# Attention's turn by row halves with values in pairs, and feed-forward's hidden block split ahead

## The reference

```
h = rmsnorm(x); z = h @ w_in          # q, k, v, forget of group A; q, k, v of group B
s = einsum(q, k) * SCALE + bias       # A: causal, bias C[t] - C[s], C = cumsum(log sigmoid(f))
p = softmax(s)                        # B: own chunk of 64 and 8 chunks before, bias by distance
o = einsum(p, v)                      # 8 heads of 64 in each group
x = x + rmsnorm(concat(rmsnorm(oa), rmsnorm(ob)) @ w_out)
hf = rmsnorm(x)
x = x + rmsnorm((silu(hf @ w_gate) * (hf @ w_up)) @ w_down)    # 1024 -> 2816 -> 1024
```

## Time and profile before

| | us |
|---|---|
| median of 3 runs | 3740.98 (3739.13 to 3746.12) |
| profiled execution | 3741.29 |
| its span | 3739.6 |
| PE busy | 3186.6 (85%) |
| weight loads busy (beside PE) | 2799.0 (75%) |
| DVE busy | 1498.0 (40%) |
| ACT busy | 1228.9 (33%) |
| POOL busy | 188.6 (5%) |

### The profile page before, as it was taken

One profiled execution on the slowest core, in us unless ns is written; L12 is line 12 of the kernel. 1 busy time (PEld: TensorE's weight loads), 2 busy tenths in 40 slices (PEclk: granted clock), 3 DMA queues, 4 the chain that ended last, 5 costly groups with the idle time before them and its releaser, 6 DMA issues. The chain is left out here.

```text
span 3739.6 us, 55132 instructions
## 1 busy us (share of the span) xinstructions
PE 3186.6 (85%) x21766; PEld 2799.0 (75%) x21766; DVE 1498.0 (40%) x2841; ACT 1228.9 (33%) x1920; POOL 188.6 (5%) x167
## 2 busy tenths in 40 slices
PE   0599999907999999745796999899899899899898
PEld 0499999806777767523585899799799799799797
DVE  4300000046656677512443443443443434434454
ACT  3111111105666667411443322222222222222333
POOL 4100000000000000000010000100100100100100
PEclk9999999958999999868898999999899999999999
DMA  2111111123211122297454334234333433433454
GB/s 96 65 71 68 70 69 46 37 36 121 67 57 31 33 76 61 68 313 277 142 162 156 131 128 158 101 125 174 105 121 137 146 118 134 146 123 129 152 185 146
DMA packets 176471, 428.39 MB, mean 115 GB/s; under 512 B 14952, under 2 KB 100512, under 8 KB 155808
## 3 DMA queue, kind: packets, MB, share of 16 engines
q1 hardware_dynamic: 154920, 399.40, 31.8%
q10 hardware_dynamic: 21392, 26.82, 2.0%
HBM read 361.45 MB, written 64.71 MB: 114 GB/s over the span
## 5 line engine op out<-in xcount | busy, mean ns | idle before, releaser
L172 PE MATMUL ffn_pg<-ffn_hh,ffn_wgh 128*128 128x384 f32 (+1 forms) x1056 | 350.7, 332 | 119.3 <-DVE ffn_hl L1662 119.3
L1590 ACT ACTIVATE ffn_wdh<-ffn_wdr 128x1024 fp32r<-128x1024 f32 x132 | 140.0, 1060 | 930.2 <-PE ffn_py L1551 930.2
L1652 DVE TENSOR_TENSOR ffn_wgl<-ffn_wgr,ffn_wgh 128x2048 fp32r<-128x2048 f32 x132 | 313.3, 2374 | 90.9 <-ACT ffn_wgh L1584 90.9
L174 PE MATMUL ffn_pg<-ffn_hh,ffn_wgl 128*128 128x384 f32 (+1 forms) x1056 | 349.6, 331 | 0.0
L173 PE MATMUL ffn_pg<-ffn_hl,ffn_wgh 128*128 128x384 f32 (+1 forms) x1056 | 349.1, 331 | 0.0
L172 PE MATMUL ffn_pu<-ffn_hh,ffn_wgh 128*128 128x384 f32 (+1 forms) x1056 | 343.7, 326 | 0.0
L173 PE MATMUL ffn_pu<-ffn_hl,ffn_wgh 128*128 128x384 f32 (+1 forms) x1056 | 343.7, 326 | 0.0
L174 PE MATMUL ffn_pu<-ffn_hh,ffn_wgl 128*128 128x384 f32 (+1 forms) x1056 | 343.7, 326 | 0.0
L1657 DVE TENSOR_TENSOR ffn_wdl<-ffn_wdr,ffn_wdh 128x1024 fp32r<-128x1024 f32 x132 | 161.8, 1226 | 435.4 <-ACT ffn_wdh L1590 435.4
L172 PEld LDWEIGHTS ffn_pg<-ffn_hh,ffn_wgh 128*128 128x128 f32 x1056 | 203.2, 192 | 126.3 <-issue 74.1
L1550 PE MATMUL ffn_py<-ffn_wdl,ffn_ah 128*128 128x512 f32 x748 | 293.1, 392 | 0.0
(11 more groups left out here) (203 smaller groups left out, 5858.7 us busy)
## 6 DMA issues: line engine op xcount, KB each, us to landing
ffn_wgr<-in_w_gu SPq DMA_DIRECT2D x132, 1024.0 KB, 4.8
ffn_wdr<-in_w_dn SPq DMA_DIRECT2D x132, 512.0 KB, 3.5
att_raw<-out_zT SPq DMA_DIRECT2D x64, 256.0 KB, 2.9
str_kr<-in_cache_ak SPq DMA_DIRECT2D x8, 2048.0 KB, 16.8
str_vr<-in_cache_av SPq DMA_DIRECT2D x8, 2048.0 KB, 15.9
out_zT<-prj_zo ACTq DMA_DIRECT2D x64, 224.0 KB
prj_raw<-in_w_slab SPq DMA_DIRECT2D x12, 1024.0 KB, 5.1
out_v<-prj_vo ACTq DMA_DIRECT2D x68, 128.0 KB, 1.8
```

Of the source, the lines that this page charges most:

```text
L172: nc.tensor.matmul(out, a_hi(k), b_hi(k), start=(k == 0), stop=False)
L174: last = nc.tensor.matmul(out, a_lo(k), b_hi(k), start=False, stop=(k == kk - 1))
L1652: nc.vector.tensor_tensor(wgl[u][:], wgr[u][:], f32(wgh[u][:]), ALU.subtract).then_inc(s_gl, 1)
```

## The change

In attention:
- `attend_order` puts the turn ahead of the scores in each step.
- `turn` takes each 128×128 block in two halves of 64 query rows, x = 0 and 1: each is a transpose with 64×128 weights and 64 moving columns, on rows 64x to 64x+64, into bank pt[x]. Both heads of a half lie in one bank, and the counter s_tr goes up once for a group and no longer once for each head.
- `copy` takes pt[x], both heads at once, into the columns 64x to 64x+64 of each tile in the new pts (3 buffers of 4 KB). DVE takes half 1 of the groups with even G, ACT all others.
- `values` and `turn_out` run only ahead of a turn with even G: the values of two groups one after the other, one and two groups further back than before.
- `turn_out` is two plain fp32 matmuls on column halves.
- On ACT the exponential of the next job's head 1 stands behind both copies of the group with g = 1 (or of the only group). `sums` has 6 buffers.

DVE's order in attention follows PE's in the same way (evict, outward, copy).

In the feed-forward block: hh and hl have two buffers. `walk` is unrolled over the blocks. The high and low halves of block b+1 are made ahead of the last step of block b, its load is issued after the second step of block b, ACT's sums of squares of block b come after the first step of block b+1, and DVE's scaling after its second step. PE waits for the low half in step 0 of a block.

```diff
         done = 0
         for x in range(parts):
             upto = -(-len(scored) * (x + 1) // parts)
+            out += turned[x:x + 1]
             out += scored[done:upto]
             done = upto
-            out += turned[x:x + 1]
     return out
 
 
...
-
-    def by_dve(e, g):
-        return e == 1 and g == 0
-
-    def copies(n, e, g, dve):
-
-        own = sum(by_dve(y, x) == dve for x in range(g + 1) for y in range(2) if (x, y) <= (g, e))
-        return (n if dve else 2 * A0[n] - n) + own
+    NPT, NSX, NSM, NOS, NRAW = 3, 3, 6, 4, 4
+
+    def by_dve(G, x):
+        return x == 1 and G % 2 == 0
+
+    def copies(G, dve):
+
+        return (G // 2 + 1) if dve else 2 * (G + 1) - (G // 2 + 1)
...
-        pts = [[m.sb(f"pts{e}{u}", [P, 512]) for u in range(NPT)] for e in range(2)]
+        pts = [m.sb(f"pts{u}", [P, 2, 4, P]) for u in range(NPT)]
-        sums = [m.sb(f"sums{u}", [P, 2]) for u in range(NSX)]
+        sums = [m.sb(f"sums{u}", [P, 2]) for u in range(NSM)]
...
-                def copied(n, e, g):
-                    if by_dve(e, g):
-                        pe.wait_ge(s_cd, copies(n, e, g, True))
-                    else:
-                        pe.wait_ge(s_ca, copies(n, e, g, False))
-
-                def turn(n, g, before):
+                def copied(G):
+                    pe.wait_ge(s_ca, copies(G, False))
+                    pe.wait_ge(s_cd, copies(G, True))
+
+                def turn(n, g):
+                    G = A0[n] + g
                     tiles = job_groups(n)[g]
                     t0 = job_tiles(n)[0]
+                    if G >= 1:
+                        copied(G - 1)
                     for e in range(2):
                         if g == 0:
                             pe.wait_ge(s_ex, 2 * n + e + 1)
-                        if before:
-                            copied(before[0], e, before[1])
                         for j, kt in enumerate(tiles):
                             c = (kt - t0) * P
-                            last = nc.tensor.transpose(pt[e][:, j * P:(j + 1) * P], sx[n % NSX][:, e, c:c + P], eye[:])
-                        last.then_inc(s_tr, 1)
+                            for x in range(2):
+                                r = slice(64 * x, 64 * x + 64)
+                                to = (4 * e + j) * 64
+                                last = nc.tensor.transpose(pt[x][:, to:to + 64], sx[n % NSX][r, e, c:c + P], eye[r, r])
+                    last.then_inc(s_tr, 1)
...
-                    nc.tensor.transpose(po[n % 2][:, P:2 * P], ot[n % 2][:], eye[:]).then_inc(s_to, 1)
+                    for x in range(2):
+                        r = slice(64 * x, 64 * x + 64)
+                        last = nc.tensor.matmul(po[n % 2][r, P:2 * P], ot[n % 2][:, r], eye[:], start=True, stop=True,
+                                                skip_group_check=True)
+                    last.then_inc(s_to, 1)
...
-                held, ended = None, None
+                held, ended = [], []
                 for what, n, g in ORDER:
                     if what == "score":
                         score(n, g)
                     else:
-                        turn(n, g, held)
-                        if ended is not None:
-                            turn_out(ended)
-                            ended = None
-                        if held:
-                            values(*held)
-                            if last_of(*held):
-                                ended = held[0]
-                        held = (n, g)
-                if ended is not None:
-                    turn_out(ended)
-                values(*held)
-                turn_out(held[0])
+                        if (A0[n] + g) % 2 == 0:
+                            for x in ended:
+                                turn_out(x)
+                            ended = []
+                            for x in held[:-1]:
+                                values(*x)
+                                if last_of(*x):
+                                    ended.append(x[0])
+                            held = held[-1:]
+                        turn(n, g)
+                        held.append((n, g))
+                for x in ended:
+                    turn_out(x)
+                ended = []
+                for x in held:
+                    values(*x)
+                    if last_of(*x):
+                        ended.append(x[0])
+                for x in ended:
+                    turn_out(x)
...
-                    if n >= NSX:
-                        act.wait_ge(s_ev, n - NSX + 1)
+                    if n >= NSM:
+                        act.wait_ge(s_ev, n - NSM + 1)
                     nc.scalar.activation(sx[n % NSX][:, e, :w], sx[n % NSX][:, e, :w], ACT.Exp, bias=nm[n % NSX][:, e:e + 1],
-                                         scale=-1.0, accum_out=sums[n % NSX][:, e:e + 1]).then_inc(s_ex, 1)
...
...
                 for what, n, g in ORDER:
                     if what == "turn":
                         more = n + 1 < NJOB
-                        copy(n, 0, g)
+                        copy(n, g, 0)
                         if more and g == 0:
                             exps(n + 1, 0)
-                        if more and g == 1:
-                            exps(n + 1, 1)
-                        copy(n, 1, g)
-                        if more and g == 0 and last_of(n, g):
+                        copy(n, g, 1)
+                        if more and g == (0 if last_of(n, 0) else 1):
                             exps(n + 1, 1)
                         if last_of(n, g):
...
-        hh = m.sb("hh", [P, KD, TM], F32R)
-        hl = m.sb("hl", [P, KD, TM], F32R)
+        hh = [m.sb(f"hh{u}", [P, KD, TM], F32R) for u in range(2)]
+        hl = [m.sb(f"hl{u}", [P, KD, TM], F32R) for u in range(2)]
...
+        def tiles_of(b):
+            return 3 if b < NBL - 1 else 2
+
+        def walk(eng, step, after_first, after_second, before_last, finish):
+
+            for b in range(NBL):
+                nt = tiles_of(b)
                 step(b, nt, 0, 0)
-                with eng.Fori(0, NJ // 2 - 1) as i:
-                    for u in (1, 0):
-                        step(b, nt, 2 * i + 2 - u, u)
+                after_first(b)
+                step(b, nt, 1, 1)
+                after_second(b)
+                with eng.Fori(1, NJ // 2 - 1) as i:
+                    for u in range(2):
+                        step(b, nt, 2 * i + u, u)
+                step(b, nt, NJ - 2, 0)
+                before_last(b)
                 step(b, nt, NJ - 1, 1)
-                last(b, nt)
-            blk(0, 3)
-            with eng.Fori(1, NBL - 1) as b:
-                blk(b, 3)
-            blk(NBL - 1, 2)
+                finish(b)
+
+        def nothing(b):
+            return None
...
+                def hidden(b):
+                    if b < NBL:
+                        after(sp, s_hl, b)
+                        sp.dma_start(hr[:, :, :tiles_of(b) * P], t["hT"][:, :, b * TM:b * TM + tiles_of(b) * P]).then_inc(s_h, 16)
...
-                walk(sp, first, step, lambda b, nt: None)
+                hidden(0)
+                walk(sp, step, nothing, lambda b: hidden(b + 1), nothing, nothing)
...
+                    if isinstance(j, int) and j == 0:
+                        pe.wait_ge(s_hl, b + 1)
...
+                def hidden(b):
+                    if b < NBL:
+                        w = tiles_of(b) * P
+                        act.wait_ge(s_h, 16 * b + 16)
+                        if b >= 2:
+                            act.wait_ge(s_pu, NJ * (b - 1))
+                        nc.scalar.activation(hh[b % 2][:, :, :w], hr[:, :, :w], ACT.Copy).then_inc(s_hh, 1)
...
+                def sums(b):
+                    if b < 0:
+                        return
...
+                hidden(0)
                 split_gate(0, 0, 0)
                 split_down(0, 0, 0)
-                walk(act, first, step, last)
+                walk(act, step, lambda b: sums(b - 1), nothing, lambda b: hidden(b + 1), evict)
+                sums(NBL - 1)
...
+                def scaled(b):
+                    if b < 0:
+                        return
...
+                hidden(0)
                 split_gate(0, 0, 0)
                 split_down(0, 0, 0)
-                walk(dve, first, step, last)
+                walk(dve, step, nothing, lambda b: scaled(b - 1), lambda b: hidden(b + 1), evict)
+                scaled(NBL - 1)
```

134 lines of the change are left out of this document (60 added, 74 removed).

## The result

| | before | after |
|---|---|---|
| median, us | 3743.14 (4 runs) | 3633.86 (4 runs, 3631.93 to 3640.15) |
| ratio, 95% interval | | 0.9712 [0.9695, 0.9728] |
| profiled execution, its span | 3741.29, 3739.6 | 3640.15, 3638.4 |
| attention of the new stream, first to last matmul | 703.9 | 683.8 |
| from there to the first matmul of the feed-forward | 496.6 | 502.2 |

What follows compares the result with a forecast made beforehand. PE was taken to set the end in both attention and feed-forward. From 3741.3 us, 98 off in the feed-forward and 108 in attention (145 of PE's work less 37 of waits) gave 3535, range 3490 to 3605.

Steps and rivals of the forecast that it cites:

- PE's work: Attention: PE's work falls 145 us: turn −84, switches −47, first loads −28, turn-out +14.
- The price of a half-turn pair: Attention: two half-height transposes cost 0.058 us in place of 0.109, 84 us off over 1648 transposes.
- Rival 1: Attention: two half-height loads go one after another, a pair costs 0.110, turning gains nothing; 3600 us, chance 0.17.
- The strided copies: Attention: strided reads and 256 B pieces cost copies nothing, at most 0.1 us each, 41 us of ACT.
- rival 4: Attention: PE's waits drop the granted clock to 0.50, the stage takes some 950 us, the kernel 3890; chance 0.03.
- What then is late: Attention: of PE's 145 us, 37 come back as waits around copies and exponentials, leaving −108.
- Rival 2: Attention: ACT's chain of copies and exponentials swallows the gain, leaving 30 to 54 us; 3600 us, chance 0.09.
- The six buffers of sums: Attention, jobs of one group: ACT's waits on the output buffer's eviction go, 2.4 us a head pair.
- Boundaries: Feed-forward: PE's waits for the low half go at 5 block boundaries, 89.4 us, plus 0.8 of matmul tail.
- The clock's 7.5 us: Feed-forward: the half-speed clock after each of 5 boundary gaps goes if PE does not stop, 1.5 us each.
- The scaling in step 2: Feed-forward: DVE's moved scaling can make a step late by 0.3 us, 2 in all; left at 0.
- Rival 3: Attention: nothing waits, PE's 145 us come in full and 2 to 10 us of old waits go; 3490 us, chance 0.05.

Runs made afterwards that it cites:

- `full_turn`: The whole change, but with the old 128×128 transposes over the whole array, a head in a bank; 0.9924 of before, 3718 us.
- `evict_between`: The whole change, but DVE evicts an ended job between the two bias passes of the last scores ahead of an even turn; 0.9594 of before.
- `values_apart`: On `between_spread`, one group's values stand ahead of the even turn and the other's behind it; 0.9505 of before, 3560.0 us.
- `half_copy`: On `between_spread`, the second head's half of every copy left out, a timing kernel only; 0.949 of before, 3552 us.
- `exp_behind`: On `evict_between`, both of ACT's copies put ahead of the exponential that stood between them; 0.9599 of before.
- `half_turn`: The kernel before with only the turn by row halves, its order, pairing, sums and feed-forward kept; 0.9965 of before, 3732 us.
- `between_spread`: On `evict_between`, DVE's feed-forward scaling spread over three steps, one row block each, in place of one step; 0.9564 of before.

## Why the prediction was wrong

Two terms of attention failed: PE's work, mis-sized, and above all the waits that it would turn into, one of which was not in the sum.

**PE's work: −145 was too much, about −100 is what the rows show.** Its busy time in the stage fell by 102 us (675.4 to 573.1), and its idle time rose by 81 (25 to 106); their difference is the 21 us that the window lost. The price of a half-turn pair, 0.058 us, is near: in the timeline above four pairs take 0.27 us, 0.11 for the first and 0.06 for each behind it. But the first pair of every group costs that 0.11, so the mean is 0.066 (2983 intervals of 0.033 us within groups, the 33 with a stop in them left out), and the turns gave some 70 us by this estimate, not 84. The change between whole array and row halves is 0.093 as said: a whole transpose is followed by values or scores after 0.202 us (before, `full_turn`) and by the next transpose after 0.109. How the other 30 us divide among switches, first loads and turn-out, no run tells. Rival 1 (loads one after another, 3600) is refuted by the pair's price, though its time is nearer to the result than the forecast's. The Trainium skill, "TensorEngine Tiling (Array Packing)", Key Properties, says that different tiles load and multiply in parallel; the trace agrees, with a pair of loads and matmuls every 0.06 us. The column price in the Trainium skill's "TensorE: Matmul & The Clock Gate", LDWEIGHTS (107 ns for 128 columns), would have given rival 1 and is not what these loads took. The strided copies taken at 0 are 0: a copy of 512 columns takes ACT 594 ns before and after, one of 384 takes 487 and 488. The clock held at a mean of 0.99, with three falls of 3.4 us (last section): rival 4 is refuted in its size. (Its 950 us for the stage do not follow from its terms: 907 of streaming and the 138 of 592 that do not stream make up to 1045. Nothing hangs on it.)

**What then is late: this step failed.** It gave back 37 us as waits; PE's idle time alone rose by 81. It has three faults, by the runs:
- *A wait that it did not list.* It walked copies, exponentials and ACT's chain, and never asked what the paired values wait for. Before, values came singly, and between the turn-out of a job and the first values two jobs on stood scores and a turn; the waits of before have no row of PE for an eviction. Pairing leaves only one group's values between them on PE, while on DVE the eviction stays behind two bias passes. It is 76 us by the loads' row, and 42 of them came back when the eviction alone was moved (`evict_between`); none was forecast. Its sign shows in the table by size: the band jobs, where every double step ends a job, became slower than before.
- *A wait that it mis-sized, by less.* Turn to turn it took 0.25 us a pair of groups, 34 us, from typical scores of 0.55 to 0.8 us. By the starts the stops ahead of turns are 44 us. In the long band jobs, which hold 96 of the 272 groups, one score group of 256 columns (0.46 us) stands there against a chain of turn, copy and release of 1.07 us (1318.65 to 1319.72), and the stop is 0.37 us on average. Covering these stops by values gives 21 us net of the added switches (`values_apart`), and shortening the copies by a third gives 25 (`half_copy`).
- *A cap put on the wrong engine.* It gave short and band jobs a floor by ACT's busy time plus 0.6 us idle. The times lie well above that floor: the jobs of two groups take 24.2 us where it had 19.2, and the long band jobs 53.1 where it had 42.6, with ACT waiting 217.9 us for turns in the stage. Moving an exponential behind both copies had no effect (`exp_behind`). Rival 2 asked the right question of the wrong engine; waits for ACT's copies took the saving only in the old order, where the half turn brought 19 us (`half_turn`).

The six buffers of sums, forecast at 2.4 us in each pair, are worth 21 us (19 forecast): right, as far as the old order goes, in which they were run.

That a saving on PE is not a saving of time is the other lesson of the runs. The half turn takes 68 us off PE's busy time in the old order and 19 off the stage; in the new one it takes off 102 and 78. The rest of the new attention costs 79 us with whole turns and 22 with half ones. In the old order the saving became waits for ACT's copies (52 us in the matmuls' row of `half_turn`, 9 before); in the new one PE's idle time changed little with the turn (81 to 106 us), so most of the saving came through.

**Feed-forward: mechanism right, one term mis-sized.** Boundaries 89.4 + 0.8 us: gone in full, 18.5 us to 0.23, none over 2 us there, and the first block keeps its wait (25.3 us, now named by the weight split). Splits ahead of the last step: hidden, at nothing, and the low half takes 3.36 us in place of the 5.49 of the earlier trace rows, since POOL's adds are no longer beside it. The clock's 7.5 us: gone, bar one fall. Start: taken at 0, is 4.6 us. The scaling in step 2 was put at 2 us in all ("a step late by 0.3"), and is 10.7 us of gaps, and half speed behind one of them: 12.9 us of DVE's work against 12.6 of step was the right sum, but the weight split stands at the end of that queue and is wanted at the start of the next step, not at its end, so PE waits for the order and not for the sum. 13 us came back when the queue was cut in three (`between_spread`). −98 against −90.

**Rest.** Rival 3 (nothing waits) is refuted. The 10 us of the middle stretch were in no case. In sum: 206 forecast = 98 + 108; found 109 in the medians, 101 between the two profiled executions: 90 + 20, 1 ahead of attention, less 10 in the untouched middle.

## What to carry over

When an edit puts two steps of one engine next to each other, write down for each of them which buffer it overwrites and where the instruction that frees it stands in the *other* engine's queue; a busy share says nothing of that. Price a saving in the loop that closes last, not in the engine's work: the same edit of the turn was worth 19 us in one order of the instructions and 78 in another. And before a large edit is judged, run its smallest piece alone: here three more buffers of sums gave all that the attention edits gave, and one moved eviction gave twice as much again.

## What the hardware showed that was not expected

- DVE and POOL beside each other: a split of 128×2048 takes DVE 4.48 us when POOL's add is under way before it, and 2.28 us when it starts 0.15 us ahead of the add, which then takes 4.37 us; two such adds with no split beside them took 5.54 together. Who starts first is not slowed, and the other ends well behind it (the split at 2322.10, the add 2.24 us later, where an add alone takes 2.77). The Trainium skill, "SBUF — State Buffer", SBUF: two separate sides, says that the pair of ports that the two share is locked for a whole instruction by whichever starts first; these rows agree, but for the half us by which the add ends earlier than a lock to the split's end would have it.
- How short a stop of PE can be ahead of a fall of the granted clock. In the profile after, the last job of each of the four forgetting pairs has a stop of 1.76 us, and in three of the four the clock was at 0.50 for 3.4 us from about the stop's end on (up to 1.2 us behind it), as here behind the stop that ended at 1270.87:

```profile
1271.60:1275.00 3.40, 3.40 (x34) 3.40 (x36) 0.29 (x1) 1.08 (x2) 0.00 (x0) 0.50 0.10 24
```

  The jobs of four groups took 38.2 us a pair in the three and 36.7 in the fourth. In the profile before the four stops there are 1.64 us and one had a fall; in `half_turn` they are 2.9 us and all four had one. The gaps of 1.3 to 1.4 us in the feed-forward had none. The one of 5.2 us there had 6.8 us at 0.50, and those of 17 to 18 us of before 17.1 to 20.5, each from within the gap on.
